# Output weights trade seats in a four-slot ring, so that other slots of the expert ring come free first

## The reference, cut to what matters

```python
z = h @ W_in + b_in                                  # 1024 x 8448
merged = sum_i sigmoid(gate_i) * (branch_i @ P_i)
x = x + merged @ W_out                               # 1024 x 1024, the items that change seats
...
hg = jnp.einsum("nd,edf->nef", t, w_gate)            # 32 experts, 1024 x 256 each
hu = jnp.einsum("nd,edf->nef", t, w_up)
a = jax.nn.silu(hg) * hu * combine[..., None]
return jnp.einsum("nef,efd->nd", a, w_down)          # 32 x 256 x 1024
```

## Time and profile before

| what | value |
|---|---|
| three timed runs | 1020.93, 1021.18, 1024.0 us; median 1021.18 |
| profiled execution, its own time | 1023.52 us |
| span of that execution, first to last instruction | 1021.3 us |
| mean granted TensorE clock, share of full speed | 0.981 |
| PE busy | 956.8 us (94%) |
| DVE busy | 560.0 us (55%) |
| ACT busy | 430.9 us (42%) |
| SP's DMA queue | 312.04 MB, 80.0% of 16 DMA engines' span |

### The profile page before, as it was taken

The page is one execution under the profiler, slowest core; times in us unless marked ns, Lnnn a source line. Parts: engine busy times, 40 slices in busy tenths (PEclk is TensorE's granted clock), DMA queues, the critical chain, the costliest instruction groups (busy, mean ns, idle before and its releaser), DMA issues.

```text
span 1021.3 us, 15602 instructions
## 1 busy us (share of the span) xinstructions
PE 956.8 (94%) x5906; PEld 669.6 (66%) x5906; DVE 560.0 (55%) x1320; ACT 430.9 (42%) x918; POOL 57.9 (6%) x74
## 2 busy tenths in 40 slices
PE   9999999999999995986999999999999999978777
PEld 7888877788886442542588888777888954434323
DVE  8666787886873231220276668787869534122212
ACT  5444566766443210211353355666764441111122
POOL 1120400000010000000003004000000100000000
PEclk9999999999999998997999999999999999989989
DMA  9975643248999999999997755332589999999996
GB/s 345 350 258 179 202 125 124 83 130 283 410 358 425 418 426 424 425 426 428 416 372 235 240 181 192 124 124 81 173 299 389 384 424 415 426 425 425 426 426 266
DMA packets 97114, 313.03 MB, mean 307 GB/s; under 512 B 13424, under 2 KB 18576, under 8 KB 74512
## 3 DMA queue, kind: packets, MB, share of 16 engines
q1 hardware_dynamic: 96704, 312.04, 80.0%
q10 hardware_dynamic: 336, 0.02, 0.0%
HBM read 310.20 MB, written 1.84 MB: 306 GB/s over the span
## 4 chain that ended last, share of the span: by engine, by line
PE 77%; DMA 13%; SPq 5%; DVE 2%; ACT 1%; issue 1%; DVEq 0%; POOL 0%; POOLq 0%; ACTq 0%
PE ps L1460 16%; PE ps L1462 15%; PE ps L1461 15%; PE ps L2088 7%; DMA arena<-in_w_expert_up_dram 5%; DMA ring_rest<-in_w_expert_down_dram 5%; SPq L498 5%; PE ps L2062 3%; DMA ring_rest<-in_w_expert_up_dram 3%; PE ps L2162 2%; PE ps L1583 2%; PE ps L2174 2%; PE ps L1595 2%; PE ps L1485 2%; PE ps L2033 1%; PE ps L1611 1%
## 5 line engine op out<-in xcount | busy, mean ns | idle before, releaser
L1112 DVE TENSOR_TENSOR split_w<-arena,split_w 128x512 fp32r<-128x512 f32 (+1 forms) x352 | 233.1, 701 | 102.2 <-ACT split_w L905 99.0
L1460 PE MATMUL ps<-split_w,split_a 128*128 128x512 f32 (+1 forms) x736 | 284.3, 386 | 0.6 <-DVE split_w L1112 0.6
L1462 PE MATMUL ps<-split_w,split_a 128*128 128x512 f32 (+1 forms) x736 | 277.1, 376 | 0.0
L1461 PE MATMUL ps<-split_w,split_a 128*128 128x512 f32 (+1 forms) x736 | 276.9, 376 | 0.0
L905 ACT CAST split_w<-arena 128x1024 fp32r<-128x1024 f32 (+1 forms) x171 | 175.9, 1031 | 178.2 <-PE ps L1462 171.6
L1460 PEld LDWEIGHTS ps<-split_w,split_a 128*128 128x128 f32 x736 | 138.5, 188 | 28.7 <-issue 3.3
L1462 PEld LDWEIGHTS ps<-split_w,split_a 128*128 128x128 f32 x736 | 138.4, 188 | 25.9
L1461 PEld LDWEIGHTS ps<-split_w,split_a 128*128 128x128 f32 x736 | 138.7, 188 | 23.1
L2317 DVE SCALAR_TENSOR_TENSOR acts<-ps,wslot,acts 128x256 f32<-128x256 f32 x16 | 7.7, 484 | 168.5 <-ACT acts L1989 145.8
L2088 PE MATMUL ps<-arena,rows 128*32 128x512 f32 x416 | 90.4, 613 | 6.0 <-DMA arena<-in_w_expert_up_dram 4.1
L2088 PE MATMUL ps<-ring_rest,rows 128*32 128x512 f32 x352 | 76.3, 641 | 13.7 <-DMA arena<-in_w_expert_up_dram 13.7
(11 more groups left out here) (291 smaller groups left out, 1081.7 us busy)
## 6 DMA issues: line engine op xcount, KB each, us to landing
arena<-in_w_in_dram SPq DMA_DIRECT2D x62, 1024.0 KB, 5.3
arena<-in_w_expert_down_dram SPq DMA_DIRECT2D x36, 1024.0 KB, 19.4
arena<-in_w_expert_gate_dram SPq DMA_DIRECT2D x34, 1024.0 KB, 24.4
arena<-in_w_expert_up_dram SPq DMA_DIRECT2D x32, 1024.0 KB, 24.1
ring_rest<-in_w_expert_down_dram SPq DMA_DIRECT2D x24, 1024.0 KB, 17.9
ring_rest<-in_w_expert_gate_dram SPq DMA_DIRECT2D x22, 1024.0 KB, 24.0
ring_rest<-in_w_expert_up_dram SPq DMA_DIRECT2D x22, 1024.0 KB, 25.6
arena<-in_w_proj_a_dram SPq DMA_DIRECT2D x8, 1024.0 KB, 5.0
```

The lines of the kernel that those rows point to most:

```text
L1112: dve.tensor_tensor(wlo[:, jj % 2, cols], half_slot(jj, w)[:, cols], whi[:, jj % 2, cols].bitcast(F32), ALU.subtract).then_inc(low_split i ...
L1460: pe.matmul(o, hi, rhs_hi, start=first, stop=False)
L1461: pe.matmul(o, hi, rhs_lo, start=False, stop=False)
L1462: return pe.matmul(o, lo, rhs_hi, start=False, stop=last)
```

## The change

The four output items change seats. The first half of w_out (items 42 and 43, steps 84 to 87) is now loaded at places 44 and 45, into ring slots 0 and 1; the second half (items 44 and 45, steps 88 to 91) at places 42 and 43, into ring slots 2 and 3. With that, ring slots 0 and 1 are read for the last time by steps 85 and 87 and slots 2 and 3 by 90 and 91, so the loads of slots 8 to 11 get other waits and another order. The load of slot 6 moves from behind the first output item to behind the third, and the third is no longer behind the wait for `gated` 8. Two pieces of JUNK move to PSUM banks, and the first square waits for four parts of the new x, where it waited for two.

```diff
-        JUNK = tuple(ps[:, 1 + q, :] if q in (1, 2) else arena[:, RING_A * SLOT:] for q in range(4))
+        JUNK = (ps[:, 3, :], ps[:, 2, :], ps[:, 3, :], arena[:, RING_A * SLOT:])
...
         def squares_act(act, nh):
-            act.wait_ge(x_done, 4 * nh + 2)
+            act.wait_ge(x_done, 4 * nh + (2 if nh else 4))
             act.wait_ge(h2t_ready, 2 * nh + 1)
             for q in (2 * nh, 2 * nh + 1):
-                if q == 1:
-                    act.wait_ge(x_done, 4)
...
-                        + [("out", r) for r in range(4)])
+                        + [("out", r) for r in (2, 3, 0, 1)])
+
+                def seat(item):
+
+                    return {42: 44, 43: 45, 44: 42, 45: 43}.get(item, item)
+
+                def ring_at(item):
+                    return seat(item) % RING
...
                             if item == 42:
                                 sp.wait_ge(gated, 4)
-                                load_ahead(2, 6)
-                            if item == 43:
+                                load_ahead(2)
+                            if item == 44:
+                                load_ahead(6)
                                 sp.wait_ge(gated, 8)
                                 load_ahead(4)
                         sp.wait_ge(gates_ready, 3)
...
+                        sp.wait_ge(low_split, 2 * 43)
+                        load_ahead(8)
                         sp.wait_ge(low_split, 2 * 44)
+                        load_ahead(9)
+                        sp.wait_ge(low_split, NARROW + 3)
+                        load_ahead(10)
+                        sp.wait_ge(low_split, NARROW + 4)
                         load_ahead(11)
-                        sp.wait_ge(low_split, NARROW + 3)
-                        load_ahead(8)
-                        sp.wait_ge(low_split, NARROW + 4)
-                        load_ahead(9, 10)
                         item_used(sp, NARROW + 2)
                         load_ahead(12, 16)
```

More of the change, by code:

```diff
@@ L646, in halved_blocks, with ring_landed @@
                     return ((w_proj_b[l], r, 4, r // 2, 0),)
-                def ring_landed(slot, item):
-                    return 16 * (item // 4 + 1 + (slot == 0 and item >= 40))
+                def ring_landed(item):
+                    at = seat(item)
+                    return 16 * (at // 4 + 1 + (at % RING == 0 and at >= 40))
                 def heads(b):
@@ L873, in narrow_slot @@
                         c, item = divmod(j - NARROW, 2)
-                        blocks = ring[:, (NARROW // 2 + item) % RING, :].rearrange("p (k n) -> p k n", k=4)
+                        blocks = ring[:, ring_at(NARROW // 2 + item), :].rearrange("p (k n) -> p k n", k=4)
                         ks = slice(2 * kk, 2 * kk + 2) if kk is not None else slice(0, 4)
@@ L880, in half_slot @@
                         n = 2 * w
-                        return ring[:, (j // 2) % RING, (j % 2) * n:(j % 2) * n + n]
+                        return ring[:, ring_at(j // 2), (j % 2) * n:(j % 2) * n + n]
                     @block.scalar
@@ L895, in high @@
                             if landed is not None:
-                                act.wait_ge(ring_in[(jj // 2) % RING], landed)
+                                act.wait_ge(ring_in[ring_at(jj // 2)], landed)
                             if used is not None:
@@ L956, in high_at @@
                                 item = NARROW // 2 + j % 2
-                                act.wait_ge(ring_in[item % RING], ring_landed(item % RING, item))
+                                act.wait_ge(ring_in[ring_at(item)], ring_landed(item))
                                 high(j, BANK, None, None)
                                 return
-                            high(j, TAIL if 64 <= j < Z_CONV else BANK, ring_landed(j // 2 % RING, j // 2), j - 1 if j < 64 else None)
+                            high(j, TAIL if 64 <= j < Z_CONV else BANK, ring_landed(j // 2), j - 1 if j < 64 else None)
                         for j in range(32, 40):
@@ L1013, in halves_at @@
                         def halves_at(j):
-                            act.wait_ge(ring_in[(j // 2) % RING], ring_landed(j // 2 % RING, j // 2))
+                            act.wait_ge(ring_in[ring_at(j // 2)], ring_landed(j // 2))
                             act.wait_ge(conv_used, j - 1)
```

## The result

The changed kernel takes **1024.3 us** (median of 20 runs, 1022.25 to 1025.82) against 1021.25 us for the kernel before (20 runs, 1019.94 to 1025.18): a ratio of 1.0028, 95% interval 1.0022 to 1.0034. It is slower by about 3.0 us, and 1.1 us above the range of the prediction.

A forecast was written before the change was run, and what follows sets the result against it. It took the expert stage as DMA-bound from SP's issue at 345.65, itself set by TensorE's own work. The terms, 2 x (0.1 - 0.2) = -0.2 us, took the median 1021.2 to 1021.0 us, range 1018.6 to 1023.2.

The forecast's parts named there:

- rival B: Casts of steps 84 and 86: items land late and delay TensorE, up to 1.0 us per layer, 1022.8 us; chance 0.17.
- three loads at 424 GB/s end at 282.6 and the fourth at 285.1: Queue after its restart at 275.2: the fourth output item, for step 86, ends transfer at 285.1 and lands at 286.3.
- 0.1 us per layer: Step 86: the fourth output item just fits, landing at 286.3 where 286.4 is allowed; cost taken as 0.1 us per layer.
- The backlog of 0.55 MB: DMA queue at SP's issue at 345.65: only 0.55 MB, or 1.3 us, of earlier loads is left.
- The dip: DMA rate behind the issue at 345.65: new bytes flow from 347.2, 0.08 MB more by 352, gaining 0.2 us per layer.
- D: Issue at 345.65: bytes flow with no delay, at most 1.7 us per layer gained, 1017.8 us; chance 0.06.
- Rival A: Expert stage: its time runs from the hole at 300, so 1.8 us per layer is won, 1017.5 us; chance 0.12.
- (1): Sign: between 300 and 307 the DMA rate is near 424 GB/s and no hole is left.
- (2): Sign: the rate falls to nearly zero for one to two microseconds just before 347, and again 504 us later.
- (3): Sign: the issue that follows quad 1's products stands within 0.3 us of 345.65.
- (4): Sign: casts 84 and 86 start within 0.5 us of 279.41 and 285.77; idle time ending on a DMA means rival B.
- (5): Sign: from quad 1's issue to the end of the experts takes as long as before, within half a microsecond.

The follow-up runs named there:

- e4: The changed kernel with slot 2's load also moved behind the third output item, so three loads stand ahead of the fourth; 1031.73 us, ratio 1.0103.
- e6: The changed kernel with third and fourth output items each loaded in two halves, casts 84 and 86 waiting for the first half only; 1021.66 us, ratio 1.0005.
- f0: The changed kernel with slot 6's load back ahead of the third output item, and the third and fourth items loaded in halves; 1021.62 us, ratio 1.0003.
- f2: f0 with quad 1's gate products put ahead of its up products, so four loads issue earlier; 1019.93 us, ratio 0.9993.
- e8: The kernel before with slot 11's load behind slot 8's wait and slot 8's behind the last one, a larger hole; 1025.14 us, ratio 1.0036.
- e2: The changed kernel with the loads of slots 6 and 4 moved behind the fourth output item; 1024.83 us, ratio 1.0036.
- e7: The kernel before with only the edits on the squares: other PSUM banks and the longer wait for x; 1020.69 us, ratio 0.9997.
- f1: The kernel before with quad 1's gate products put ahead of its up products, so four loads issue earlier; 1020.24 us, ratio 0.9990.

## Why the prediction was wrong

The mechanism that decided was that of rival B, late seats, which had 0.17, and only 0.06 beyond 0.3%. B looked for it at step 84's cast, with step 86's behind it; it came at step 86 alone, and beyond the size that B gave it.

- **The step that failed: "three loads at 424 GB/s end at 282.6 and the fourth at 285.1".** In the frame of this trace, 0.69 us later, the item should have landed at 287.0; it landed at 287.94. The rate was wrong. Summed from 275.9 on, by the rows above, 275 to 277 moved 0.34 MB and 277 to 283 another 2.58, so that three loads (3.15 MB) ended near 283.8, 0.5 us late. Then the fourth moved at 299 and 347 GB/s, at DMA shares of 0.89 and 0.99, and needed 3.2 us in place of 2.5: with the same 1.2 us behind it 287.0 + 1.2 = 288.2, a quarter of a microsecond more than measured. The engines were occupied and still moved a fifth less than 424. The kernel before has the same in this place:

```profile
250.00:262.00 12.00, 12.00 (x55) 9.92 (x54) 8.44 (x14) 8.37 (x9) 0.00 (x0) 1.00 1.04 403
...
280.00:286.00 6.00, 5.99 (x29) 4.67 (x28) 5.65 (x10) 2.71 (x5) 0.00 (x0) 1.00 0.98 341
286.00:292.00 6.00, 6.00 (x32) 5.07 (x30) 4.62 (x8) 2.84 (x4) 0.00 (x0) 1.00 0.99 360
```

  The 369 GB/s of the earlier trace rows are no such rate, but a mean over a slow start (255 GB/s up to 250) and over 400 behind it. Why it is less at 280 to 292 stays open: the packets had 2.0 and 3.0 KB on the mean there and 2.3 KB at 250 to 262, so their size alone does not order the rates. The earlier trace rows held the landing itself: the 6.3 us of the issue at 784.6 are those of the load in this very place in the kernel before, behind slot 4's (5.7 us in layer 0), where step 86 did not wait for it. The prediction left 6.2 us from issue to landing, with slot 6's load ahead as well, and used the 6.3 for the third item alone.
- **The term "0.1 us per layer"** measured 1.0 to 1.4 us, and 2.25 in one layer of one trace. "The upper bound of both is 1.0 us per layer" rested on a late third item; the third was never late in the changed kernel. The upper bound had to be put to the fourth item's own transfer. e4, e6 and f0 show that the late item makes this term: by a larger dose, by its removal and by its removal with another order.
- **The slack of 0.67 us** behind the cast was 0.4: a cast 1.5 us late made TensorE 1.06 us late.
- **"The queue is simply dry 1.8 us earlier, at about 345.2": wrong.** At 345 to 347 the rate is 422. The closed hole came back at 306 to 310 and 322 to 325, where SP waits for TensorE. But the conclusion, that the closed hole is worth nothing, was right, for another reason than the one given: f0 closes the hole with TensorE on time and wins nothing, and f2 shows that it does not pay even with an earlier issue.
- **The backlog of 0.55 MB** stands, within the 0.1 MB of a rounded rate: by the issue f0 has moved 0.2 MB more than the kernel before, and its queue still moves 420 GB/s in the last microsecond ahead of the issue, so the closed hole did not empty it.
- **The dip: gain of 0.2 us per layer.** It brought no gain and no loss: over 6.35 us the two layers of the four traces have 357 to 406 GB/s before and 364 to 413 with the change, 385 on the mean in both. The 364 of the first trace against the 395 of the earlier trace rows is scatter. D, with its quick restart, is seen nowhere: behind the issue into the dry queue at 274.4 the rate of 275 to 277 is 168 GB/s. At 242.21, in the kernel before, the first packets move at 243.2, 1.0 us behind the start of SP's issue and 0.6 us behind its end. The Trainium skill (DMA: Bandwidth & Descriptors, Specifications) gives about 0.6 us to the first byte; counted from the end of the issue, the trace agrees. The prediction held that figure against the later time at which the full rate would have had to begin, so its "more than twice that" compares two things.
- **Rival A** fell for an earlier fill, and e8 shows that it holds for a later one: the fill is worth nothing while the queue would run dry anyway, and counts once it would not (nearly in full in e8, by some three quarters in e2).
- **The third item, slot 11 and the squares** cost nothing, as forecast: cast 84 is in its place, and e7 is no change.
- Of the list of what would show it, (1) held, (2) failed, (3) failed (347.40, which is 1.06 us late with the later start taken off), (4) began B at step 86, and (5) held: 423 GB/s over 159.6 us, where the earlier trace rows have 424 over 159.35. The sign against it, the products at 285.69 a microsecond late, did not come: they stand at 286.43, 0.05 us from their old place with the later start taken off, since step 86 comes behind them.
- **"About 0.3% is what a measurement of this kernel can tell"** was too coarse: 20 runs of each kernel tell 0.28% from no change.

## What to carry to other kernels

Take the transfer time of a late load from rows of the same kind of load in the same stretch, not from the best rate in the trace; a DMA share of 0.99 to 1.01 stood beside 347, 375 and 424 GB/s here. The landing of the load that already had this place in the queue is the nearest row of all. A reordering that has an item issued at its last possible moment (5.5 to 5.8 us ahead of its use, with 4.7 us the least that one of these items, whole, needed in any trace) has no room for anything ahead of it in the queue: cast from the first half of it, or leave it where it was. A hole in the DMA stream, once closed, opened again at the next places where SP waits for TensorE, and moving one later gate did not make it pay (f2); whether moving all of them would was not tried.

## What was not expected of the hardware

Between two bursts the queue loses more than its idle time: with loads issued 2 us before, 283 to 285 went at 299 GB/s at a share of 0.89, and after a dry spell the first 2 us went at 168 at a share of 0.76. In e2, behind the same two loads and with the next ones issued 8 us before, 291 to 293 went at 267 GB/s at a share of 0.98. A stall can cost more than its length: in e4 each layer lost 1.7 us more at a granted clock of 0.50 behind it. Splitting a product of 512 columns into two of 256 cost TensorE 0.1 us at most: f1 issues its second four loads at 345.69, 103.54 us behind the start of its fill, where it was 103.44 before.
